# The grouped-query projection of the sample tiles as two times seven block products

## The chip, the cores and the metric

The kernel runs on one core of a Trainium2 chip. The metric is the device time of one execution, in microseconds. Before the change it was 1909.35 us (median of 3 runs, 1907.31 to 1909.38).

## What is computed

Two layers of a transformer step on 384 tokens of width 1024: one tile of 128 prompt tokens and two tiles of 128 sample tokens. Everything is float32. Cut to what matters here:

```python
z = h @ p['w_in']            # (384, 1024) @ (1024, 6048): all projections of the layer
(c_q, c_kv, k_pe, gq, gk, gv, dq, dk, dv, g_mla, g_gqa, g_diff) = jnp.split(z, splits, axis=-1)
gq = rmsnorm(gq.reshape(b, t, 8, 64), p['gqa_q_norm'])     # grouped-query: 512 columns of q,
gk = rmsnorm(gk.reshape(b, t, 2, 64), p['gqa_k_norm'])     # 128 of k, 128 of v: 768 in all
gv = gv.reshape(b, t, 2, 64)
o_mla, o_gqa = attend(q, k_mla, v_mla), attend(gq, gk_all, gv_all)      # 8 and 8 heads
a1, a2 = attend(dq[..., :64], ...), attend(dq[..., 64:], ...)           # 4 heads, two maps
merged = sigmoid(g_mla) * (o_mla @ w_br_mla) + sigmoid(g_gqa) * (o_gqa @ w_br_gqa) + ...
x = x + gate1 * (merged @ p['w_out'])
x = x + gate2 * expert_choice_ffn(h, p)                    # 16 experts, 3 matrices of 1024x1024 each
```

The change is in how the 768 grouped-query columns of `z` are computed for the 256 sample tokens.

## The kernel before

**Stages of a layer.** First the modulation and the normalised tokens, transposed into `hT` (8 blocks of 128 features by 384 tokens). Then the projection `c0` (latent attention), the grouped-query projection `c1` of the prompt tile, the q and v projections, and after that a loop over 16 attention jobs (`JOBS`: 8 `mla`, 4 `gqa`, 4 `diff`). Then the merge, the output projection, routing, and 16 experts, whose weights (12 MB each) stream through the 8 slots of `ring` and 10 more slots in `arena`.

**The job loop.** TensorE in job i does `scores(i)`, `prep(i + 1)` (transposes for the next job), `values(i - 1)`, then the filler list `FILL[i]`, then `turn_probs(i)` (transposes of the probabilities). VectorE does the maxima, ScalarE the exponentials, VectorE the normalisation; the filler gives TensorE work meanwhile. I write F0, F1, ... for the stretch of filler in job 0, 1, ... The order is written out by hand in `FILL`: F0 and F1 hold the `c1` projections of sample tiles 1 and 2 (`("c1", t, h)`, h the half of 384 columns), F2 and the lists after it other projections of `z`, the modulation blocks `ada` and their transposes `adat`, and the block products below.

**Block products.** `product` (L1849) and `two` (L1870) already compute other projections by seven products instead of eight: both operands are split into 2x2 blocks, and sums and differences of blocks are multiplied (M5, M1, M2, M6, M3, M7, M4, in this order). Each product is 4 accumulating matmuls of 192 columns. GpSimd makes the sums of blocks: `tile_sums` (L733) those of the tokens, `column_sums` (L743) those of the weights. ScalarE copies M5 and M1 out of their banks, VectorE adds the other five into place (L1339 to L1350). A plain projection (`project`, L1812) is 8 accumulating matmuls of 384 columns for a tile and a half, and ScalarE copies it out (L996).

**PSUM banks.** There are 8. Banks 0 to 3 hold scores. Banks 4 and 5 are used by `prep`: 4 for keys (copied out by VectorE, signal `prep_dve`), 5 for queries (copied out by ScalarE, `prep_act`); a filler may borrow them after that copy, and must be out before `turn_probs` takes them. Banks 6 and 7 are free for fillers. Every use is a "user", and `user_banks` gives it the bank used longest ago, by the numbers in `latest`; the user then waits until the former holder was copied out (`user_act` or `user_dve`).

**Weights.** SyncE's queue loads 1 MB units in the order of `PLAN` into the ring; a load waits until TensorE has counted the slot as used. The four `c1` units are released in the last projection of tile 2 (F1), and their slots take `ada` units that are used in F3.

**Signals.** `sq2_ok` comes after the squares of the latent projection, whose scratch `SQG` lies over columns 3072 to 4991 of `arena`; ScalarE squares the grouped-query rows into the same scratch at the end of F1 (L1076), with VectorE's mean and GpSimd's scaling after it (`rg_ok`).

## Time and profile before

| What | Value |
|---|---|
| median of 3 runs | 1909.35 us (1907.31 to 1909.38) |
| the profiled execution, its own time | 1909.12 us |
| its span, first to last instruction | 1907.3 us |
| TensorE matmul busy | 1760.6 us (92%) |
| VectorE / ScalarE / GpSimd busy | 671.7 / 325.6 / 320.7 us |
| mean granted TensorE clock | 0.986 |
| DMA | 541.14 MB, mean 284 GB/s |

The span ends 1.8 us short of the profiled execution's time; what lies around it is the start and the end of the program. A row of the trace names a line, an engine, an operation and its tiles. A float32 matmul shows as two records on PE and two weight loads on PEld, so that "x32" on PE is 16 matmuls. Arrows name what the engine waited for. The busy time of PE overlaps with the next records at its ends by some 0.1 us, so durations of stretches are best taken from start to start.

### The profile page before, as it was taken

The page shows a single profiled execution, that of the slowest core. Times are in us where ns is not written, and L with a number is a line of the kernel's source. Part 1 is how long each engine was busy: PE and PEld are TensorE (multiplying, and loading weights), DVE is VectorE, ACT ScalarE, POOL GpSimd, SP SyncE. Part 2 cuts the span into 40 slices and gives each one's busy share as a digit, 9 for nine tenths or more (in the row PEclk, how much of TensorE's full clock was granted, in tenths as well). Part 3 has the DMA queues.
Part 4 walks back from the last instruction along what each step waited for, and adds up shares of the span by engine and source line. Part 5 has one row for each costly group of instructions (what it writes and reads, how often), then busy time and mean ns, then how long its engine had stood idle before and what let it go on. Part 6 is the DMA issues. An engine that isn't in the chain of part 4 may idle for free.

```text
span 1907.3 us, 21463 instructions
## 1 busy us (share of the span) xinstructions
PE 1760.6 (92%) x8548; PEld 972.3 (51%) x8548; DVE 671.7 (35%) x1375; ACT 325.6 (17%) x811; POOL 320.7 (17%) x349
## 2 busy tenths in 40 slices
PE   6999999999999988889889999999999999898886
PEld 3656777894533323233255587778844333332322
DVE  1135556752412212122132455567424131221212
ACT  2232223320301001010032322222112010100101
POOL 0216455330000000000002437533200000000000
PEclk9999999999899999999999999999999999999999
DMA  9235132139499999999961642313448999999997
GB/s 389 84 143 235 70 130 78 67 136 412 184 428 427 431 428 429 430 429 429 427 246 71 236 159 94 122 46 131 196 202 331 429 430 428 430 429 429 428 429 294
DMA packets 58289, 541.14 MB, mean 284 GB/s; under 512 B 7048, under 2 KB 7496, under 8 KB 14416
## 3 DMA queue, kind: packets, MB, share of 16 engines
q1 hardware_dynamic: 56656, 535.65, 67.7%
q0 software_dynamic: 1536, 4.13, 0.6%
q8 instruction: 69, 1.13, 0.2%
q14 instruction: 28, 0.23, 0.0%
HBM read 536.54 MB, written 3.21 MB: 283 GB/s over the span
## 4 chain that ended last, share of the span: by engine, by line
PE 78%; DMA 12%; DVE 4%; SPq 3%; ACT 2%; issue 1%; DVEq 0%; ACTq 0%
PE banks L2300 25%; PE banks L1863 10%; PE banks L1825 8%; DMA arena<-in_w_exp 7%; PE banks L1915 7%; PE banks L2219 4%; PE banks L1717 4%; PE banks L1887 4%; SPq L678 3%; PE banks L2379 3%; DMA ring<-in_w_exp 3%; PE banks L2088 1%; PE banks L2275 1%; DMA ring<-in_w_att 1%; PE banks L1772 1%; PE banks L2029 1%
## 5 line engine op out<-in xcount | busy, mean ns | idle before, releaser
L2300 PE MATMUL banks<-arena 128*64 128x512 f32 x1680 | 378.9, 595 | 31.5 <-DMA arena<-in_w_exp 19.7
L2300 PE MATMUL banks<-ring,arena 128*64 128x512 f32 x1392 | 314.9, 598 | 21.0 <-DMA ring<-in_w_exp 10.9
L2300 PEld LDWEIGHTS banks<-arena 128*64 128x64 f32 x1680 | 116.6, 137 | 272.2 <-issue 217.5
L2300 PEld LDWEIGHTS banks<-ring,arena 128*64 128x64 f32 x1392 | 97.7, 138 | 220.9 <-issue 179.4
L1654 DVE TENSOR_TENSOR arena<-banks,arena 32x512 f32<-32x512 f32 (+1 forms) x128 | 87.9, 687 | 266.0 <-PE banks L2300 264.6
L1825 PE MATMUL banks<-ring,arena 128*128 128x384 f32 (+1 forms) x512 | 161.7, 476 | 1.8 <-ACT arena L930 1.8
L1717 PE MATMUL banks<-arena 128*128 128x128 f32 (+3 forms) x740 | 106.2, 278 | 31.5 <-DVE arena L1639 18.6
L1717 PEld LDWEIGHTS banks<-arena 128*128 128x128 f32 (+3 forms) x740 | 83.0, 140 | 94.0 <-issue 41.3
L1825 PEld LDWEIGHTS banks<-ring,arena 128*128 128x128 f32 x512 | 97.2, 192 | 61.7 <-issue 2.7
L1915 PE MATMUL banks<-arena,ring 128*128 128x384 f32 x384 | 126.8, 488 | 0.0
L1138 ACT ACTIVATE arena<-banks 128x512 f32<-128x512 f32 x32 | 19.1, 597 | 511.7 <-PE banks L2300 511.7
L806 POOL COPY arena<-arena 128x32 f32<-128x32 f32 x4 | 0.8, 211 | 604.6 <-ACT arena L1036 604.3
L1863 PE MATMUL banks<-ring 128*128 128x192 f32 x544 | 97.0, 328 | 0.8 <-DVE arena L1319 0.8
L1915 PEld LDWEIGHTS banks<-arena,ring 128*128 128x128 f32 x384 | 72.2, 190 | 48.8 <-issue 1.5
L1639 DVE TENSOR_TENSOR arena<-arena,banks 128x512 f32<-128x512 f32 x32 | 22.0, 688 | 207.4 <-PE banks L2300 207.4
L1863 PEld LDWEIGHTS banks<-ring 128*128 128x128 f32 x544 | 88.9, 190 | 3.5 <-DVE arena L1319 1.3
L2219 PE MATMUL banks<-ring,arena 128*128 128x512 f32 x192 | 86.5, 604 | 1.2 <-DVE arena L1319 1.2
L956 ACT ACTIVATE arena<-banks,arena 128x384 f32<-128x384 f32 x144 | 71.4, 508 | 91.0 <-DVE arena L1259 91.0
L1636 DVE TENSOR_TENSOR arena<-banks,arena 128x512 f32<-128x512 f32 x32 | 22.1, 691 | 171.8 <-ACT arena L1138 171.8
L908 POOL TENSOR_TENSOR arena<-arena 128x1024 f32<-128x1024 f32 x1 | 2.4, 2365 | 443.3 <-DVE arena L1664 443.3
L2379 PE MATMUL banks<-arena 128*128 128x512 f32 (+1 forms) x112 | 54.4, 642 | 21.7 <-DVE arena L1654 18.6
L1257 DVE TENSOR_REDUCE arena<-banks 128x1 f32<-128x384 f32 x144 | 58.5, 461 | 29.0 <-PE banks L2022 14.6
(251 smaller groups left out, 2051.5 us busy)
## 6 DMA issues: line engine op xcount, KB each, us to landing
arena<-in_w_exp SPq DMA_DIRECT2D x69, 2048.0 KB, 30.6
ring<-in_w_exp SPq DMA_DIRECT2D x69, 2048.0 KB, 29.5
ring<-in_w_att SPq DMA_DIRECT2D x80, 1024.0 KB, 6.7
arena<-in_w_exp SPq DMA_DIRECT2D x72, 1024.0 KB, 27.2
ring<-in_w_exp SPq DMA_DIRECT2D x36, 1024.0 KB, 14.1
ring<-in_w_att SPq DMA_DIRECT2D x26, 768.0 KB, 8.2
arena<-in_w_att SPq DMA_DIRECT2D x12, 1024.0 KB, 11.5
ring<-in_w_att SPq DMA_DIRECT2D x8, 672.0 KB, 15.2
```

The costliest lines, as they stand in the source:

```text
L678: sp.dma_start(span(group), a["w_exp"][l, c0:c1].rearrange("(p n) -> p n", p=P))\
L956: ins = nc.scalar.activation(PB[:, b, lo:hi], PS[:, 2 * m + bank, c:c + hi - lo], ACT.Exp, scale=SCALE[kind], bias=NB[:, b, r:r + 1], accu ...
L1257: ins = nc.vector.reduce_max(MX[:, b, r:r + 1], PS[:, 2 * m + bank, c:c + w], AX)
L1654: ins = nc.vector.tensor_tensor(y[32 * e:32 * e + hi - lo, BF * h:BF * h + BF], PS[64 * h + lo:64 * h + hi, 5], G2[64 * h + lo:64 * h + hi ...
L1717: return pe.transpose(out, src, IDT[0:rows, 0:rows])
L1825: ins = pe.matmul(ps[:, 0:width], hT[:, k, P * t:P * t + P], slots[n][:, c0:c0 + width], start=k == 0, stop=k == KC - 1)
L1863: ins = pe.matmul(ps[:, 0:HALF], lhs[:, k], rhs[:, k], start=k == 0, stop=k == 3)
L1887: ins = pe.matmul(ps[:, 0:HALF], lhs[:, k], rhs[k], start=k == 0, stop=k == 3)
L1915: ins = pe.matmul(ps[:, 0:TOK], w[:, k, P * (c % 4):P * (c % 4) + P], o[:, k], start=k == 0, stop=k == 3)
L2219: ins = pe.matmul(ps, MG[:, k, P * t:P * t + P], slots[n][:, c0:c0 + BF], start=k == 0, stop=k == KC - 1)
L2300: ins = pe.matmul(PS[64 * h:64 * h + 64, bank], lhs(k), slots[i][:, c0:c0 + BF], start=k == 0, stop=k == KC - 1)
L2379: ins = pe.matmul(combine_bank(g, n)[:, c:c1], w, YS[0 if t else 1][:, BF * h + c:BF * h + c1], start=True, stop=True)
```

## The change

The four `c1` projections of the sample tiles go out of F0 and F1. In their place stand two groups of seven block products, `("two", 2, q, m)`, q the half of 384 output columns: q = 0 in F0, q = 1 in F1. GpSimd gets two new pieces of work in each layer: `tile_sums(l, 1)` ahead of the rotary key, and `grouped_sums(l, q)`, the weight sums, q = 0 before the stores of the latent projection, q = 1 after the rotation of q. The sums of q = 1 go to the same four tiles (`WG`, arena columns 3072 to 6143) as those of q = 0, each after the product of q = 0 that reads it. ScalarE's squares wait for VectorE's last product of q = 1 instead of ScalarE's own last copy. In `user_banks` the estimates for when banks 4 and 5 become free change, and `("adat", 1)` is put in bank 4.

```diff
@@ fill table and bank assignment
-for _t in range(1, NT):
-    FILL[_t - 1] += [("c1", _t, h) for h in range(2)]
...
+GROUPED = 2
+for _q in range(2):
+    FILL[_q] += [("two", GROUPED, _q, m) for m in PRODUCTS]
...
         if left and left == len(FILL[i]):
-            latest[4], latest[5] = n - 1.6, n - (1.7 if i == 7 else 1.5)
+            late = 0 if i and values_of(i - 1) else 1
+            latest[4], latest[5] = n - 1.6 + late, n - 1.5 + late
             holder.pop(4, None), holder.pop(5, None)
-        b = min((4, 5, 6, 7) if left > 2 else (6, 7), key=lambda x: latest[x])
+        b = 4 if user == ("adat", 1) else min((4, 5, 6, 7) if left > 2 else (6, 7), key=lambda x: latest[x])
@@ backbone: operand tiles
-        TS = (SUMS[0][0], SUMS[0][1], at(25568, 4, P), SUMS[0][2])
+        TS = [(SUMS[0][0], SUMS[0][1], at(25568, 4, P), SUMS[0][2]),
+              (at(23264, 4, P), at(23776, 4, P), at(24288, 4, P), SUMS[0][2])]
+        WG = tuple(at(3072 + 4 * HALF * n, 4, HALF) for n in range(4))
@@ GpSimd
-            def tile_sums(l):
-
-                pool.wait_ge(user_mm.s, user_mm.at(l, USER_AT["gate", 0, 3, M4] + 1))
+            def tile_sums(l, early):
+
+                if early:
+                    pool.wait_ge(ht_act.s, ht_act.at(l, 4 * NT))
+                    pool.wait_ge(ht_dve.s, ht_dve.at(l, 4 * NT))
+                    pool.wait_ge(mod_t.s, mod_t.at(l, 1))
...
+            def grouped_sums(l, q):
+
+
+                units = [place[l, ("c1", u)] for u in range(4)]
+                for i, first, load, _ in units:
+                    pool.wait_ge(filled[first].s, 16 * load)
+                b11, b12 = ([columns(units[u][0], q, h) for u in range(2)] for h in range(2))
+                b21, b22 = ([columns(units[u][0], q, h) for u in range(2, 4)] for h in range(2))
+                t1, t2, t3, t4 = ([t[:, 0:2], t[:, 2:4]] for t in WG)
+                if q == 0:
+                    pool.wait_ge(sq2_ok.s, sq2_ok.at(l, 1))
+                else:
+                    pool.wait_ge(user_mm.s, user_mm.at(l, USER_AT["two", GROUPED, 0, M5] + 1))
+                pool.tensor_tensor(t1[0], b12[0], b11[0], ALU.subtract)
+                link(pool.tensor_tensor(t1[1], b12[1], b11[1], ALU.subtract), l)
+                if q:
+                    pool.wait_ge(user_mm.s, user_mm.at(l, USER_AT["two", GROUPED, 0, M6] + 1))
+                pool.tensor_tensor(t2[0], b22[0], t1[0], ALU.subtract)
+                link(pool.tensor_tensor(t2[1], b22[1], t1[1], ALU.subtract), l)
+                if q:
+                    pool.wait_ge(user_mm.s, user_mm.at(l, USER_AT["two", GROUPED, 0, M4] + 1))
+                for u in range(2):
+                    pool.tensor_tensor(t3[u], b22[u], b12[u], ALU.subtract)
+                pool.tensor_tensor(t4[0], b21[0], t2[0], ALU.subtract)
+                pool.tensor_tensor(t4[1], b21[1], t2[1], ALU.subtract).then_inc(two_ok.s, 1)
...
-                    pool.wait_ge(mod_t.s, mod_t.at(l, 1))
+                    pool.wait_ge(user_mm.s, user_mm.at(l, USER_AT["two", GROUPED, 1, M4] + 1))
...
+                tile_sums(l, 1)
                 pool.wait_ge(user_act.s, user_act.at(l, evacuated(USER_AT["c0", 2, 1])))
...
+                grouped_sums(l, 0)
 
                 pool.wait_ge(za_ok.s, za_ok.at(l, 1))
...
+                grouped_sums(l, 1)
                 pool.wait_ge(rg_ok.s, rg_ok.at(l, 1))
...
@@ ScalarE and VectorE
-                        act.wait_ge(user_act.s, user_act.at(l, evacuated(USER_AT["c1", 2, 1])))
+                        act.wait_ge(user_act.s, user_act.at(l, evacuated(USER_AT["c1", 0, 1])))
+                        act.wait_ge(user_dve.s, user_dve.at(l, evacuated(USER_AT["two", GROUPED, 1, M4])))
                         nc.scalar.activation(SQG, ZG[:, :, 0:640], ACT.Square).then_inc(sqg_ok.s, 1)
...
-                    c = 768 * b + TOK * u
-                    first, second = ZD[:, 1, c:c + TOK], ZD[:, 2, c:c + TOK]
+                    c, z = (TOK * u, ZG) if b == GROUPED else (768 * b + TOK * u, ZD)
+                    first, second = z[:, 1, c:c + TOK], z[:, 2, c:c + TOK]
@@ TensorE: two() and fill()
-                units = [arrived(l, "c2", 4 * f + u) for u in range(4)]
+                early = int(f == GROUPED)
+                units = [arrived(l, "c1", u) if early else arrived(l, "c2", 4 * f + u) for u in range(4)]
                 if m == M5:
-                    pe.wait_ge(tiles_ok.s, tiles_ok.at(l, 1))
-                    pe.wait_ge(two_ok.s, two_ok.at(l, 2 * f + q + 1))
+                    pe.wait_ge(tiles_ok.s, tiles_ok.at(l, 2 - early))
+                    pe.wait_ge(two_ok.s, two_ok.at(l, q + 1 if early else 2 * f + q + 3))
                 a11, a12, a22 = hT[:, 0:4, P:2 * P], hT[:, 4:8, P:2 * P], hT[:, 4:8, 2 * P:TOK]
                 b11, b21, b22 = ([columns(units[u + k // 2], q, h)[:, k % 2] for k in range(4)]
                                  for u, h in ((0, 0), (2, 0), (2, 1)))
-                t1, t2, t3, t4 = ([t[:, k] for k in range(4)] for t in WT[q])
-                s1, s2, s3, s4 = TS
+                t1, t2, t3, t4 = ([t[:, k] for k in range(4)] for t in (WG if early else WT[q]))
+                s1, s2, s3, s4 = TS[early]
...
-                    project(l, key, [("c1", u) for u in range(4)], ZG_W, 384, 384 * key[2], key[1],
-                            key[1:] == (2, 1))
+                    project(l, key, [("c1", u) for u in range(4)], ZG_W, 384, 384 * key[2], 0, False)
```

Four more numbers follow from this: `DVE_LINKS` 139 to 143, `POOL_LINKS` 58 to 64, and the counts of `tiles_ok` and `two_ok` (2 and 6), with the waits in `two` that go by them.

**TensorE, F0** (job 0 of a layer, between the transposes for job 1 and those of the probabilities of job 0). Before:

```order
L1717 MATMUL banks<-arena 96x128 x3
L1825 MATMUL banks<-ring,arena 128x384 x16
L1717 MATMUL banks<-arena 128x128 x7
L2020 MATMUL banks<-arena 128x384
L2021 MATMUL banks<-arena 128x128
L2022 MATMUL banks<-arena 128x384
```

Now:

```order
L1756 MATMUL banks<-arena 96x128 x3
L1927 MATMUL banks<-arena 128x192 x4
L1927 MATMUL banks<-ring,arena 128x192 x8
L1927 MATMUL banks<-arena 128x192 x4
L1927 MATMUL banks<-ring,arena 128x192 x4
L1927 MATMUL banks<-arena 128x192 x8
L1756 MATMUL banks<-arena 128x128 x7
```

Sixteen matmuls of 384 columns gave way to 28 of 192; F1 reads the same.

**GpSimd, from the rotation of q to the scaling of the grouped-query rows**, with the signals each instruction waits for. Before:

```order
L731 TENSOR_TENSOR arena<-arena 128x8x32 [waits pool_chain]
L835 TENSOR_TENSOR arena<-arena 128x640 [waits qrope_ok,rg_ok]
L836 TENSOR_TENSOR arena<-arena 128x512 [waits pool_chain]
L838 TENSOR_TENSOR arena<-arena 128x128
L835 TENSOR_TENSOR arena<-arena 128x640 [waits pool_chain]
```

Now:

```order
L735 TENSOR_TENSOR arena<-arena 128x8x32 [waits pool_chain]
L765 TENSOR_TENSOR arena<-ring 128x384 [waits filled7,filled6,user_mm,filled1,filled5]
L766 TENSOR_TENSOR arena<-ring 128x384
L769 TENSOR_TENSOR arena<-ring,arena 128x384 [waits user_mm,pool_chain]
L770 TENSOR_TENSOR arena<-ring,arena 128x384
L774 TENSOR_TENSOR arena<-ring 128x384 [waits user_mm,pool_chain]
L774 TENSOR_TENSOR arena<-ring 128x384
L775 TENSOR_TENSOR arena<-ring,arena 128x384
L776 TENSOR_TENSOR arena<-ring,arena 128x384
L873 TENSOR_TENSOR arena<-arena 128x640 [waits qrope_ok,rg_ok]
```

The eight additions of q = 1 stand between them, with three waits for TensorE (`user_mm`).

**TensorE, F7** (job 7, the products of the first gate), with the signals. Before:

```order
L1863 MATMUL banks<-ring 128x192 [waits tokens_ok,sums_ok,filled4,user_dve]
L1863 MATMUL banks<-ring 128x192 x3
L1863 MATMUL banks<-arena,ring 128x192 [waits filled4,prep_act]
L1863 MATMUL banks<-arena,ring 128x192 x3
L1863 MATMUL banks<-arena,ring 128x192 [waits filled4,prep_dve]
L1863 MATMUL banks<-arena,ring 128x192 x3
L1863 MATMUL banks<-ring 128x192 [waits filled4,user_dve]
```

Now:

```order
L1902 MATMUL banks<-ring 128x192 [waits tokens_ok,sums_ok,filled4,user_dve]
L1902 MATMUL banks<-ring 128x192 x3
L1902 MATMUL banks<-arena,ring 128x192 [waits filled4,user_dve]
L1902 MATMUL banks<-arena,ring 128x192 x3
L1902 MATMUL banks<-arena,ring 128x192 [waits filled4,prep_dve]
L1902 MATMUL banks<-arena,ring 128x192 x3
L1902 MATMUL banks<-ring 128x192 [waits filled4,prep_act]
```

The product M1 no longer waits for ScalarE's copy of bank 5 (`prep_act`); the fourth product, M6, has that wait now.

## Rows read from the trace of the kernel before

**Rows 1.** The page: DMA busy tenths, 40 slices of 47.7 us.

```profile
DMA  9235132139499999999961642313448999999997
```

**Rows 2.** Windows: stretch, length, busy us per engine, granted clock, DMA share, GB/s.

```profile
488.00:508.00 20.00, 17.65 (x61) 8.64 (x59) 10.84 (x31) 3.94 (x8) 0.00 (x0) 0.91 0.00 1
484.00:524.00 40.00, 37.05 (x171) 22.52 (x170) 20.39 (x63) 11.84 (x24) 0.00 (x0) 0.83 0.35 138
1424.00:1464.00 40.00, 35.90 (x216) 21.43 (x216) 21.21 (x66) 11.96 (x25) 4.01 (x8) 0.91 0.72 273
```

**Rows 3.** Timeline, TensorE, F0 and F1 of layer 0: start, us, work [idle before].

```profile
99.85 10.48 PE L1825 MATMUL banks<-ring,arena 128*128 128x384 f32 x32
110.17 0.93 PE L1717 MATMUL banks<-arena 128*128 128x128 f32 x7
...
114.49 10.49 PE L1825 MATMUL banks<-ring,arena 128*128 128x384 f32 x32
...
124.82 0.93 PE L1717 MATMUL banks<-arena 128*128 128x128 f32 x7
```

**Rows 4.** Chain that ended last, by time: 56 matmuls of `two` in F8.

```profile
221.31 18.20 PE banks L1887 x112
```

**Rows 5.** Timeline and waits, GpSimd: rotation of q, and the scaling's wait.

```profile
88.04 0.72 POOL L724 TENSOR_TENSOR arena<-arena 128x256 f32<-128x256 f32 x1 [17.72 <-ACT arena L1052]
...
POOL arena L835 <- DVE arena L1453: 41.1, 1, 41.1
```

**Rows 6.** Timeline after F7: TensorE goes on, GpSimd wakes, sums of four adds.

```profile
204.64 1.15 PE L1717 MATMUL banks<-arena 128*128 128x128 f32 x9
...
204.89 1.27 POOL L738 TENSOR_TENSOR ring<-arena 128x512 f32<-128x512 f32 x1 [15.72 <-PE banks L1863]
...
222.65 1.96 POOL L761 TENSOR_TENSOR arena<-ring 128x384 f32<-128x384 f32 x2
...
225.52 1.00 POOL L763 TENSOR_TENSOR arena<-ring,arena 128x384 f32<-128x384 f32 x1
```

**Rows 7.** Timeline after F1: squares, ScalarE's copy of probabilities, TensorE.

```profile
125.53 1.80 ACT L1076 ACTIVATE arena<-arena 128x1920 f32<-128x1920 f32 x1
...
127.24 0.46 ACT L1083 COPY arena<-banks 128x384 f32<-128x384 f32 x1
...
127.75 0.53 PE L1717 MATMUL banks<-arena 128*96 128x128 f32 x3 [0.49 <-ACT arena L1083]
```

**Rows 8.** Timeline, TensorE, F5 of layer 0: M5; M1, M2; M3; M7, M4.

```profile
167.19 1.47 PE L1863 MATMUL banks<-ring 128*128 128x192 f32 x8
...
168.84 2.87 PE L1863 MATMUL banks<-arena,ring 128*128 128x192 f32 x16 [0.18 <-DVE arena L1268]
...
172.84 1.46 PE L1863 MATMUL banks<-arena 128*128 128x192 f32 x8
...
174.31 2.87 PE L1863 MATMUL banks<-ring 128*128 128x192 f32 x16
```

**Rows 9.** Timeline, F7 of layer 0: M5; VectorE's key copies; M1, M2.

```profile
193.84 1.47 PE L1863 MATMUL banks<-ring 128*128 128x192 f32 x8
...
194.61 2.79 DVE L1274 COPY arena<-banks 64x512 f32<-64x512 f32 x4
...
196.74 2.87 PE L1863 MATMUL banks<-arena,ring 128*128 128x192 f32 x16 [1.43 <-ACT arena L967]
```

**Rows 10.** Timeline, TensorE, F4: `ada` 2 in layer 0; its end in layer 1.

```profile
158.09 2.80 PE L1796 MATMUL banks<-ring,arena 128*32 128x256 f32 x48 [1.28 <-ACT arena L979]
161.81 1.07 PE L1796 MATMUL banks<-ring,arena 128*32 128x256 f32 x16 [0.92 <-DMA ring<-in_w_att]
...
1100.77 0.70 PEld L1796 LDWEIGHTS banks<-ring,arena 128*32 128x32 f32 x16 [0.16 <-DMA ring<-in_w_att]
```

**Rows 11.** Timeline: one GpSimd add and one small VectorE multiply beside each other's work.

```profile
158.63 2.73 POOL L794 TENSOR_TENSOR ring<-ring 128x512 f32<-128x512 f32 x1 [3.13 <-issue]
...
209.62 0.62 DVE L1259 TENSOR_SCALAR arena<-arena 128x3 f32<-128x3 f32 x1
```

More of the change, by code:

```diff
@@ L399, in packed_vectors @@
     return out
-DVE_LINKS = 139
-POOL_LINKS = 58
+DVE_LINKS = 143
+POOL_LINKS = 64
 def backbone(nc, a):
@@ L731, in rotate @@
                 return pool.tensor_tensor(z, t1, t2, ALU.add)
-            def tile_sums(l):
-                pool.wait_ge(user_mm.s, user_mm.at(l, USER_AT["gate", 0, 3, M4] + 1))
+            def tile_sums(l, early):
[4 more added lines that the diff above has]
+                else:
+                    pool.wait_ge(user_mm.s, user_mm.at(l, USER_AT["gate", 0, 3, M4] + 1))
                 a11, a12, a21, a22 = hT[:, 0:4, P:2 * P], hT[:, 4:8, P:2 * P], hT[:, 0:4, 2 * P:TOK], hT[:, 4:8, 2 * P:TOK]
-                s1, s2, s3, s4 = TS
+                s1, s2, s3, s4 = TS[early]
                 link(pool.tensor_tensor(s1, a21, a22, ALU.add), l)
@@ L741, in tile_sums @@
                 pool.tensor_tensor(s4, a12, s2, ALU.subtract).then_inc(tiles_ok.s, 1)
+            def grouped_sums(l, q):
[7 more added lines that the diff above has]
+                    pool.wait_ge(sq2_ok.s, sq2_ok.at(l, 1))
+                else:
+                    pool.wait_ge(user_mm.s, user_mm.at(l, USER_AT["two", GROUPED, 0, M5] + 1))
[11 more added lines that the diff above has]
+                pool.tensor_tensor(t4[1], b21[1], t2[1], ALU.subtract).then_inc(two_ok.s, 1)
             def column_sums(l, f, q):
```

6 lines of the change are left out of this document (3 added, 3 removed).

## The prediction

> **What bounds the kernel now.** I read the 40 slices first. The DMA row has two long runs of 9, the experts of each layer, and low digits between them [rows 1]. So there are two kinds of stage: attention, where TensorE's own queue sets the pace, and experts, where the weight stream does. An edit in attention pays only if the stream behind it starts earlier too. Between the two, from 488 to 508 us, the DMA share is 0.00 [rows 2]: all slots that may be filled are full, and the stream waits for TensorE to use some. So it starts when attention and routing are done, and what attention gains should reach the end one for one. The second view is the chain by time with the timeline of TensorE in F0 and F1, where the projections stand back to back [rows 3]; the reader should see that start-to-start times there hold no idle. The third is the timeline of the later fills, where short waits sit inside the products [rows 8 to 10].
>
> **The fills themselves.** F0 takes 110.17 - 99.85 = 10.32 us, F1 124.82 - 114.49 = 10.33 [rows 3]: 16 matmuls of 384 columns at 0.645. In F8 the same kind of products, 56 matmuls of 192, take 18.20 us [rows 4], 0.325 each, 1.30 a product, so 28 take 9.10. Saved: 2 x (10.32 - 9.10) = 2.45 us a layer. It is nearly the whole of the eighth that seven products for eight leave out; the short matmuls cost next to nothing extra.
>
> The Trainium skill ("TensorE: Matmul & The Clock Gate", Back-to-back issue gap) speaks against that: in a stream of weight loads and matmuls it gives about 81 ns for 128 columns and 131 for 512, so half the columns would cost far more than half the time. The trace disagrees: 0.325 against 0.645 us. The rival "short matmuls" below has this direction, with a bound from the rows.
>
> **Do the products of F0 and F1 wait?** M2 borrows bank 4 and M6 bank 5, 2.6 and 3.9 us into the fill. In F7 bank 5 came free 196.74 - 193.84 = 2.9 us into it [rows 9], and in F5 bank 4 168.84 - 167.19 = 1.65 us into it [rows 8]; both come in time. M3 and M7 take over the banks of M5 and M1, M4 that of M3, two products earlier each. The copies and adds are ScalarE's and VectorE's, hidden as those of the gate products are. Cost 0; if VectorE came late in M3's add, M4 would wait by as much.
>
> **GpSimd.** The token sums are four adds at the size of L738, 1.27 us [rows 6]: 5.1 us, ahead of the rotary key, while GpSimd has nothing else. The eight adds of q = 0 take 2 x 3.87 = 7.7 us, with 3.87 from 222.65 to 225.52 + 1.00 for four [rows 6]. They stand before the stores and the rotation of q; GpSimd had 17.72 us of idle there [rows 5]. With each add doubled they would still fit. So 0; behind them wait only the two stores and that rotation, which wakes on ScalarE's last copy at 88.0 anyway.
>
> The sums of q = 1 are the tight place. Their t3 and t4 may be written only after M4 of F0, and M5 of F1 waits for all four tiles. From the end of the fill to M5 there are 114.49 - 110.17 = 4.32 us of other TensorE work [rows 3]. GpSimd wakes 0.25 us after TensorE goes on (204.64 to 204.89) and needs 3.87 for four adds [rows 6]: 4.12, and a signal back of about 0.1 us or a little more. M5 starts then or some tenths later. I take 0.1 us a layer. Lower bound 0. Upper: an add that meets VectorE's work took 2.73 us instead of 1.27 [rows 6, 11]; two of four such would make it 2.9 late, one 1.4. The scaling behind these adds is not delayed: it waited 41.1 us for VectorE [rows 5].
>
> The Trainium skill ("SBUF — State Buffer", Who interferes with whom) says VectorE and GpSimd share a port pair under an exclusive lock: the loser blocks for the whole instruction. The trace agrees: the 2.73 us add, and a three-column multiply of VectorE that took 0.62 us beside a GpSimd add [rows 11]. By that rule the small multiply before job 1's exponentials loses about half a microsecond too, off TensorE's path, since the fill covers it.
>
> **The squares.** After F1 ScalarE does 1.8 us of squares from 125.53, then the copy at 127.24 for which TensorE idles 0.49 us at 127.75 [rows 7]. The squares started 0.71 us after the fill's end (124.82, behind the copy of the last projection). Now they wait for VectorE's last add of 192 columns. VectorE should wake as GpSimd does, 0.25 us after the fill [rows 6], and I give the add 0.35, half of the 0.70 that one of four key copies of 512 columns takes [rows 9]: 0.6 us after the fill. Gain about 0.12 a layer; bounds 0 and 0.49.
>
> **The banks of the later fills.** F5: M1 started at 168.84 where 167.19 + 1.30 = 168.49 was possible, waiting for VectorE's key copy in bank 4; now M1 is in bank 7 and only M2 needs bank 4, later than that copy: 0.35. M7 started at 174.31, with 172.84 + 1.30 = 174.14 possible, as its bank was M6's, emptied by VectorE just before; now it is M1's: 0.17 [rows 8]. Together 0.52.
>
> F7: M1 waited 1.43 us for ScalarE's copy of bank 5 [rows 9]. Now M1 has bank 6 and does not wait, but M2 has bank 4 as before, and VectorE's four key copies end at 194.61 + 2.79 = 197.40. So the next wait stands right behind: M2 starts at 197.46 instead of 196.74 + 1.30 = 198.04. Gain 0.58, not 1.43.
>
> F4: `ada` 2 waited 1.28 us for ScalarE's copy of the values of job 3 [rows 10], since its bank had held them; now its bank was `ada` 1's. But its last quarter then waits for weights: 0.92 us in layer 0, and in layer 1 the weight load still waited 0.16 us for DMA at 1100.77 [rows 10]. These loads are issued as `ada` 1 frees slots, so their arrival does not move. I take 0; the bounds are 0 and 1.28 a layer. The earlier release of the `c1` slots doesn't help: the loads that it starts are used two jobs later.
>
> **The sum.** A layer: 2.45 - 0.10 + 0.12 + 0.52 + 0.58 = 3.57; two layers 7.1 us. The profiled execution took 1909.12 us: 1902.0. Its time is 0.23 below the median of the runs, so I forecast 1902.2.
>
> **Rivals.**
>
> *Short matmuls.* Each matmul has a fixed cost that doesn't shrink with its columns, and these products have 28 where the projections had 16. At the far end a short one costs what a long one does, 28 x 0.645 = 18.1 us a fill instead of 9.1: four fills make 36 us, 1938. It costs the whole gain from 0.325 + 7.1 / 112 = 0.39 us a matmul. [Rows 4] speak against it, with the same shapes at 0.325. Chance 0.01.
>
> *The sums make F1 wait.* If one or two adds of q = 1 are held up, M5 is 1.4 to 2.9 us late a layer: 1904.8 to 1907.8. For it: adds beside VectorE at [rows 11]. Against: in those 4 us VectorE mostly reads banks, and its large multiplies fall into the middle of the fills. Chance 0.12.
>
> *The gain is swallowed at the expert stage.* The clock granted to TensorE was 0.83 from 484 to 524 us in layer 0 and 0.91 over the same stretch of layer 1 [rows 2], after idle stretches in routing: 40 x 0.17 = 6.8 and 40 x 0.09 = 3.6 us of full-speed work lost. So the same work loses 3 us more or less by how its idle falls. A layer that goes from one to the other moves the time by up to 3 us, either way: 1899 or 1905. Chance of the bad side 0.12, of the good side 0.1.
>
> *F4 pays after all*, if the loads come earlier: up to 2.6 us more, 1899.6. Chance 0.07.
>
> *Slower than before.* GpSimd and VectorE lock each other out in F0 and F1: every one of the four adds after M4 takes 2.73 us as at [rows 11]. Then the tiles are ready at 0.25 + 10.9 = 11.2 us, 6.9 after TensorE wants them, and each layer loses 6.9 - 3.6 = 3.3 us: 1915.7. It decides from 3.7 us of lateness a layer on, where the change breaks even; that takes three of the four adds held up by VectorE. Chance 0.03.
>
> *The order is not what it says*: no sign, the listing of the instructions shows the 28 matmuls and the additions where I put them.
>
> **Chances.** Main forecast 0.55, with its own range of 1900.5 to 1903.7. Change and no change differ by 0.2%, 3.8 us, the least that runs of this kernel can tell: faster means below 1905.5. That holds the main case, the good sides, half of the waits in F1 and most of the bad clock: 0.82. Within 0.2%: 0.14. Slower: 0.04, with room for what I don't see. The range runs from the good clock or F4's gain to the upper end of the late sums.
>
> **What would show it.** In the profile after: F0 at 9.1 us start to start and F1 too; in F1 M5 with a wait for GpSimd of under 0.5 us; L765 to L776 on GpSimd with adds near 1.0 us; no wait of M1 in F5 and F7, but one of about 1.0 us of M2 in F7 for VectorE's key copies; `ada` 2 with a longer wait for DMA and the same end; layer 1 beginning some 3.6 us earlier. Wrong would be: M5 of F1 over 1.5 us late, an expert stream that starts no earlier than before, or `ada` 2 ending earlier.

## The result

The changed kernel took 1896.83 us (median of three runs, 1896.20 to 1899.92) against 1909.35 before: ratio 0.9942, 95% interval 0.9924 to 0.996. The profiled execution took 1896.20, with a span of 1894.4. The forecast was 1902.2, and its range began at about 1899, the good clock; so this is below the range. Two more comparisons, with five runs of the changed kernel each, gave 1901.03 against 1908.88 (ratio 0.9963, 0.995 to 0.9975) and 1901.38 against 1908.85 (0.9961, 0.9949 to 0.9974). All 15 runs of the changed kernel have a mean of 1900.6, all 65 of the kernel before 1908.9: 8.4 us less, with a 95% interval of about 1.5 to either side. So there are two questions: where the 8 us are, and why the first three runs showed 12.5.

### The stages of the profile after

The rows below are all of TensorE's timeline in layer 0 of the changed kernel (start, us, work, idle before with its releaser). First F0 and the start of F1, beside [rows 3]:

```profile
97.50 1.47 PE L1927 MATMUL banks<-arena 128*128 128x192 f32 x8
98.80 2.76 PE L1927 MATMUL banks<-ring,arena 128*128 128x192 f32 x16
...
106.60 0.93 PE L1756 MATMUL banks<-arena 128*128 128x128 f32 x7
...
110.93 1.52 PE L1927 MATMUL banks<-arena 128*128 128x192 f32 x8
112.29 2.76 PE L1927 MATMUL banks<-ring,arena 128*128 128x192 f32 x16
...
120.09 0.93 PE L1756 MATMUL banks<-arena 128*128 128x128 f32 x7
```

F0 takes 106.60 - 97.50 = 9.10 us and F1 120.09 - 110.93 = 9.16, where they took 10.32 and 10.33. M5 of F1 starts 4.33 us after the end of F0 as before, and takes 1.36 us to the next product, 0.06 longer than the 1.30 of the others. GpSimd's last sums are as close as this:

```profile
106.91 1.95 POOL L774 TENSOR_TENSOR arena<-ring 128x384 f32<-128x384 f32 x2 [1.83 <-PE banks L1927]
108.83 0.99 POOL L775 TENSOR_TENSOR arena<-ring,arena 128x384 f32<-128x384 f32 x1
109.78 0.99 POOL L776 TENSOR_TENSOR arena<-ring,arena 128x384 f32<-128x384 f32 x1
```

They end at 110.77, 0.16 us before M5. The longest of the eight adds of q = 1 takes 1.11 us; none is stretched to 2.73 as the one at [rows 11] was. Next the squares, F4, F5 and F7, beside [rows 7 to 10]:

```profile
122.96 0.53 PE L1756 MATMUL banks<-arena 128*96 128x128 f32 x3 [0.43 <-ACT arena L1122]
...
146.63 1.06 PE L1811 MATMUL banks<-ring,arena 128*32 128x512 f32 x8 [0.48 <-DMA ring<-in_w_att]
...
152.63 2.80 PE L1835 MATMUL banks<-ring,arena 128*32 128x256 f32 x48
156.58 1.07 PE L1835 MATMUL banks<-ring,arena 128*32 128x256 f32 x16 [1.15 <-DMA ring<-in_w_att]
...
161.97 1.47 PE L1902 MATMUL banks<-ring 128*128 128x192 f32 x8
163.27 2.76 PE L1902 MATMUL banks<-arena,ring 128*128 128x192 f32 x16
...
168.47 2.76 PE L1902 MATMUL banks<-ring 128*128 128x192 f32 x16
171.07 0.93 PE L1756 MATMUL banks<-arena 128*128 128x128 f32 x7
...
187.90 1.47 PE L1902 MATMUL banks<-ring 128*128 128x192 f32 x8
189.20 1.46 PE L1902 MATMUL banks<-arena,ring 128*128 128x192 f32 x8
191.51 1.57 PE L1902 MATMUL banks<-arena,ring 128*128 128x192 f32 x8 [0.84 <-DVE arena L1313]
...
198.11 1.15 PE L1756 MATMUL banks<-arena 128*128 128x128 f32 x9
```

The reader should see four things. The wait behind the squares is 0.43 where it was 0.49. F4 has lost its wait for ScalarE (1.28), but the wait for weights behind it has grown from 0.92 to 1.15, and F3 has one of 0.48 that it did not have. F5 has no wait and takes 9.10 (9.82 before). In F7 M1 goes at once and M2 waits 0.84 for VectorE's key copies: 10.21 instead of 10.80.

From the start of F0 to the end of F7 that is 198.11 - 97.50 = 100.61 us where it was 204.64 - 99.85 = 104.79: 4.18 less. Layer 1 took 103.66 and now takes 99.94 (1032.16 to 1132.10): 3.7 less. Together 7.9 us. The stages behind pass it on one for one. In layer 0 the routing matmuls that stood at 494.72 are at 488.16, which is the 6.5 us by which F7 ended earlier. So the other 12.9 - 7.9 = 5 us of the span are not in the projections at all.

### Where the other 5 us are

The first half of them is there before the first grouped-query product: it starts at 97.50 instead of 99.85, although nothing ahead of it on TensorE was changed. The windows show the reason for most of it. The columns are stretch, length, busy us by engine, granted clock of TensorE, DMA share, GB/s. The kernel before:

```profile
20.00:40.00 20.00, 15.99 (x84) 8.33 (x77) 5.58 (x19) 3.48 (x9) 0.00 (x0) 0.83 1.01 414
```

The changed kernel:

```profile
20.00:40.00 20.00, 17.18 (x93) 8.54 (x86) 5.62 (x19) 5.32 (x14) 0.00 (x0) 1.00 1.02 418
```

A mean of 0.83 over 20 us says that a third of them was granted the lower of the two levels, 1.2 instead of 2.4 GHz; the changed kernel shows 1.00, none. From the first sample-tile matmul to the first product they took 65.87 and 64.18 us. Ahead of that matmul 24 transposes took 3.39 and 2.84 us. The second place is routing: up to the four transposes at 507.97 and 499.88 it took 13.24 and 11.73 us (from 494.72 and 488.16).

The third is late in the experts of layer 1, and it isn't the clock. From 1602.58 in the kernel before (1590.91 now) it took 53.55 and 52.26 us, with a granted clock of 1.00 in both; what differs is the wait for weights, first before and then now:

```profile
1639.87 3.65 PE L2300 MATMUL banks<-ring,arena 128*64 128x512 f32 x16 [0.33 <-DMA ring<-in_w_exp]
1644.70 3.65 PE L2300 MATMUL banks<-arena 128*64 128x512 f32 x16 [1.18 <-DMA arena<-in_w_exp]
```

```profile
1631.73 3.65 PE L2339 MATMUL banks<-arena 128*64 128x512 f32 x16 [0.43 <-DMA arena<-in_w_exp]
```

Behind it a stretch at half speed made 29.0 us of 27.3 in the kernel before (from 1763.41, now 1750.33), but the 101.4 us that follow are 103.2 now, since the weights are waited for again: that half speed had cost next to nothing by the end. In all, 0.66 us lie ahead of the first sample-tile matmul (0.55 of them in those transposes), 1.69 between it and the first product, 1.5 in routing and 1.3 in the experts of layer 1, less 0.2 in those of layer 0. Whether this belongs to the change or to the execution was the question for the experiments.

The windows of [rows 2] in the changed kernel say little by themselves, since their stretches now hold work that stood 7 to 12 us later:

```profile
484.00:524.00 40.00, 37.04 (x182) 21.36 (x180) 20.79 (x65) 12.24 (x25) 0.00 (x0) 0.87 0.51 209
1424.00:1464.00 40.00, 35.58 (x229) 19.67 (x230) 16.29 (x47) 9.74 (x20) 4.01 (x8) 0.91 0.86 350
```

The clock is 0.87 and 0.91, against 0.83 and 0.91. The DMA row of the page answers to [rows 1]: its two runs of 9 have the same number of slices, so the expert stages are as long as they were to within a slice, 47 us.

```profile
DMA  9246222149499999999961642312548999999997
```

### The profile page after: what moved, and what is told of

Its sections match the earlier page's. It is cut to its first block, busy times and chain, and to the rows that moved or that the text cites. A ratio compares the mean times of both kernels' runs of the same rounds, so it can differ in the third digit from the quotient of the medians.

```text
span 1894.4 us, 21814 instructions
## 1 busy us (share of the span) xinstructions
PE 1750.6 (92%) x8644; PEld 981.5 (52%) x8644; DVE 686.7 (36%) x1403; ACT 323.5 (17%) x811; POOL 361.6 (19%) x389
## 3 DMA queue, kind: packets, MB, share of 16 engines
q8 instruction: 70, 1.15, 0.2%
## 4 chain that ended last, share of the span: by engine, by line
PE 77%; DMA 12%; DVE 4%; SPq 3%; ACT 2%; issue 1%; DVEq 0%; ACTq 0%
PE banks L2339 25%; PE banks L1902 10%; DMA arena<-in_w_exp 8%; PE banks L1955 7%; PE banks L1864 6%; PE banks L1927 6%; PE banks L1756 4%; PE banks L2258 4%; SPq L682 3%; PE banks L2418 3%; DMA ring<-in_w_exp 3%; DMA ring<-in_w_att 2%; PE banks L2127 2%; PE banks L2314 1%; PE banks L2068 1%; PE banks L1811 1%
## 5 line engine op out<-in xcount | busy, mean ns | idle before, releaser
L1864 PE MATMUL banks<-ring,arena 128*128 128x336 f32 (+1 forms) x384 | 118.1, 468 | 1.8 <-ACT arena L968 1.8
L1864 PEld LDWEIGHTS banks<-ring,arena 128*128 128x128 f32 x384 | 72.3, 190 | 45.1 <-ACT arena L968 2.3
```

The lines of the kernel that those rows point to most:

```text
L1864: ins = pe.matmul(ps[:, 0:width], hT[:, k, P * t:P * t + P], slots[n][:, c0:c0 + width], start=k == 0, stop=k == KC - 1)
```

## The experiments

All ratios are to runs of the kernel before on the same chip. The stage times are start to start on TensorE, as above.

### The two kernels again

No edit; each was run a second time, and the changed one a third.

> The kernel before, unchanged. The mechanism theory (all that is systematic happens between the first grouped-query product and the end of the grouped-query projection; the rest of the difference between the two first profiles is where the granted TensorE clock happened to dip): ratio 1.000 to the kernel before, and this profile need not show the clock of 0.59 at 24 to 28 us and of 0.76 and 0.81 at 32 to 40 us again; first grouped-query matmul at 98 to 100 us. The systematic theory (the start is slower in the old program itself): that matmul again at 99.85 and the first sample-tile matmul at 33.98.

Measured: ratio 1.000 (0.9992 to 1.0009), 1909.47 us. The first sample-tile matmul is at 33.30, the first grouped-query fill at 97.67. That is 2.2 us earlier than in the first profile of the same program (and 0.3 earlier than the expected 98), so what the systematic theory wanted to see again is gone. Its F0 took 11.82 instead of 10.32, since half speed now fell there.

> The changed kernel, unchanged. Mechanism theory: 7.5 to 8.5 us less than the kernel before in the stretches of the two projections (104.79 and 103.65 to about 100.3 and 99.9), and a total between 1898 and 1902, since the other 5 us of the first comparison were the clock's: ratio 0.9955 to 0.997. Systematic theory: ratio 0.993 to 0.9945 again (1896 to 1899), with the first grouped-query matmul at 97.5 and the routing stretch 1.5 us shorter once more.

Measured: ratio 0.9963, 1901.03 us. The projections took 101.43 and 99.87, F0 of layer 0 among them 10.39, with half speed in it. The first product starts at 99.63, routing takes 13.24. The two projections are 7.1 us shorter, just under the expected 7.5 to 8.5, with 1.3 us of half speed in F0. So the mechanism theory holds, and the rival doesn't: neither the start nor routing is faster because of the change.

> The changed kernel once more, unchanged, for a third set of times and a third profile. Where the first comparison (12.5 us by medians, 12.9 by spans) and the second (7.9 us) differ, the theory is that the stretches at half of TensorE's clock fell elsewhere. It expects 7 to 9 us less than the kernel before (ratio 0.9953 to 0.9963), the stage times of layer 1 as in the two other profiles within 0.1 us (fills 9.10 and 9.17, F5 9.10, F7 10.21, sum 99.9), and every stage that is longer than in the other profiles by over 0.2 us under a half-speed stretch or a DMA wait. Rival (the first comparison was the true size): ratio 0.9935 and a mean granted clock of 0.988 or more in all runs.

Measured: ratio 0.9961, 1901.38 us; F0 10.48 with half speed in it, F1 9.16, F5 9.10, F7 10.22, the projection of layer 1 99.88, routing 13.24. All this was expected. One stage was not: the first sample-tile matmul is at 34.55, where it is at 33.3 and 33.4 in the two other profiles, and neither a low granted clock nor a wait for weights accounts for it. Up to 24.3 us this profile and the first one of the changed kernel agree to 0.03 us. Then come 24 transposes, here and in the first profile of the changed kernel:

```profile
26.17 3.92 PE L1756 MATMUL banks<-arena 128*128 128x128 f32 x24
```

```profile
26.01 2.84 PE L1756 MATMUL banks<-arena 128*128 128x128 f32 x24
```

And the window over them here:

```profile
25.00:30.00 5.00, 5.00 (x32) 3.68 (x24) 0.00 (x0) 0.00 (x0) 0.00 (x0) 1.00 1.02 420
```

The first of these transposes start 0.21 us apart, those from 28.35 on 0.11, and the granted clock reads 1.00 for both. So TensorE can run at half pace at the start of the program without a sign of it in that column.

### The parts alone

`banks_only` is the kernel before with these lines of the new one, and no grouped-query products (the `min` is written out in the change above):

```
+            late = 0 if i and values_of(i - 1) else 1
+            latest[4], latest[5] = n - 1.6 + late, n - 1.5 + late
+        b = 4 if user == ("adat", 1) else min(...)
```

> The kernel before with only the new rules for the accumulator banks of the fillers (no grouped-query products). Mechanism theory: F5 and F7 lose their waits (0.52 to 0.72 and 0.58 us per layer), F4 trades its wait of 1.28 us for a DMA wait of 1.14 (0 to 0.15), so 2.2 to 2.9 us less in the two stretches and a ratio of 0.9985 to 0.9989. Rival (F4's wait goes as well, since only the DMA's luck kept it): 4.5 to 5 us less, ratio 0.9975. Rival (banks cost through the squares and sums that now come later): 0 to 1 us less.

Measured: ratio 0.9987 (0.9978 to 0.9996), 1906.64 us. F5 takes 9.10 in both layers and F7 10.21, as in the changed kernel: 0.72 + 0.59 = 1.31 a layer. F3 and F4 together did not become shorter (18.48 in layer 0, with part of F4 at half speed; 17.10 in layer 1, where it was 16.96).

`products_only` is the changed kernel with the old bank rules from slot 2 on:

```
-            late = 0 if i and values_of(i - 1) else 1
-            latest[4], latest[5] = n - 1.6 + late, n - 1.5 + late
+            late = 1 if i < 2 else 0
+            latest[4], latest[5] = n - 1.6 + late, n - (1.7 if i == 7 else 1.5) + late
...
-        b = 4 if user == ("adat", 1) else min(...)
+        b = min(...)
```

> The changed kernel with the old rules for the banks of every filler from the third on: only the products of slots 0 and 1 and their sums are new. Mechanism theory: the two fills shorten by 1.2 us each, so 4.7 to 4.9 us less in the two stretches, ratio 0.9974 to 0.9976, and 1.5 per layer slower than the changed kernel in F5 and F7. If fills and banks together are the whole, this one and banks_only add up to the changed kernel within 1 us. Systematic theory: each of them shows part of the further 5 us, outside the two stretches, and their sum reaches 12.

Measured: ratio 0.9973 (0.9964 to 0.9982), 1903.75 us. F0 of layer 0 takes 9.10, F1 9.17 and 9.16; F5 and F7 have their old 9.82 and 10.80, which is 1.3 us a layer more than in the changed kernel (expected: 1.5), with the old wait of M1:

```profile
191.75 2.87 PE L1902 MATMUL banks<-arena,ring 128*128 128x192 f32 x16 [1.43 <-ACT arena L1005]
```

The two parts by medians are 5.1 and 2.2 us, 7.4 together, where the whole is 7.5 to 7.9 in the repeats. Each of these is good to some 2 us, so it is the stage times that show fills and banks to add up; neither part contains the further 5 us.

### F4 alone

`adat_only` is the kernel before with one line changed (which of the banks 6 and 7 later fillers get shifts with it):

```
-        b = min(...)
+        b = 4 if user == ("adat", 1) else min(...)
```

> The kernel before with one change: the accumulator bank of the transposed modulation tile is 4, as in the changed kernel (the choice between 6 and 7 of later fillers shifts with it). The prediction put this edit at nothing, since a DMA wait stands behind the ScalarE wait of 1.28 us at 158.09. Theory: the ScalarE wait goes and the DMA wait at the last 16 matmuls grows to about the sum, F3 and F4 together stay at 18.1 to 18.5 in layer 0 and 16.9 to 17.0 in layer 1, ratio 0.9995 to 1.0005. Rival: F4 pays, 0.5 to 1.28 us less in layer 0. If the products are what lets the weights of F4 come sooner (17.2 to 17.7 with them in three profiles, 18.1 to 18.5 without in three), this one is to stay on the side without.

Measured: ratio 1.0006 (0.9997 to 1.0015), 1910.18 us. TensorE's timeline in F4 of layer 0, for this kernel:

```profile
155.91 2.80 PE L1796 MATMUL banks<-ring,arena 128*32 128x256 f32 x48
161.17 1.32 PE L1796 MATMUL banks<-ring,arena 128*32 128x256 f32 x16 [2.46 <-DMA ring<-in_w_att]
```

In `before_again`, the same program but for this bank:

```profile
157.41 2.80 PE L1796 MATMUL banks<-ring,arena 128*32 128x256 f32 x48 [1.28 <-ACT arena L979]
161.35 1.07 PE L1796 MATMUL banks<-ring,arena 128*32 128x256 f32 x16 [1.14 <-DMA ring<-in_w_att]
```

1.28 + 1.14 = 2.42 became 2.46. The removed wait comes back as a wait for weights that were behind it, to a few hundredths. F3 and F4 of layer 0 together took 18.60, a little over the expected 18.1 to 18.5; the last row shows 1.32 us where 1.07 is full speed. In layer 1 they took 17.47 instead of 16.96, over the expected 17.0: the wait of 1.29 us went, and one of 1.47 for weights came, with matmuls ahead of it that took 2.98 instead of 2.80. So nothing was gained in either layer, and the ratio is just above the expected 1.0005.

### GpSimd's sums at F1

`sums_late` makes the third of the four sums of q = 1 (`t3`, two adds) twice:

```
+                if q:
+                    pool.tensor_tensor(t3[0], b22[0], b12[0], ALU.subtract)
+                    link(pool.tensor_tensor(t3[1], b22[1], b12[1], ALU.subtract), l)
                 for u in range(2):
                     pool.tensor_tensor(t3[u], b22[u], b12[u], ALU.subtract)
```

> The changed kernel, with GpSimd doing the third of the operand sums of the second grouped-query product twice (two more adds of 128 x 2 x 192 and one more link in each layer), so that the last sum is ready later by about 1.9 us. The prediction had put the last product of F1 0.05 us behind the sums, and the profile of the changed kernel shows that wait at 0.06 us. Theory (the sums have no slack at F1): M5 waits for GpSimd, and F1 grows from 9.17 by 1.5 to 2.1 us in each layer, 3 to 4.2 us in all, ratio 1.5 to 2.2 thousandths above the changed kernel's. Rival (the pages' small wait has slack behind it, since M1 could go first or the adds overlap): F1 grows by under 0.5 us.

Measured: ratio 0.9978 (0.9969 to 0.9987), 1905.10 us, against 0.9961 for the changed kernel in the same series: 1.7 thousandths, within the expected 1.5 to 2.2. The sums end at 116.89 + 0.99 = 117.88, first view, and TensorE takes the product up 0.15 us later, second view:

```profile
116.89 0.99 POOL L779 TENSOR_TENSOR arena<-ring,arena 128x384 f32<-128x384 f32 x1
```

```profile
115.69 0.49 PE L1759 MATMUL banks<-arena 128*96 128x128 f32 x3
118.03 1.54 PE L1930 MATMUL banks<-arena 128*128 128x192 f32 x8 [1.85 <-POOL arena L779]
```

From the end of F0 to M5 of F1 it is 6.34 us in both layers instead of 4.33: 2.01 us more. The sums end 6.19 us after F0 instead of 4.17: 2.02 more. So they have no slack, as the prediction had it. The expectation looked for the lateness inside F1; it stands ahead of M5, between F0 and F1, and F1 itself still takes 9.17.

### The other bank in F7

`other_bank_f7` is the changed kernel with the old constant for slot 7, so that M2 takes bank 5 and M6 bank 4:

```
-            latest[4], latest[5] = n - 1.6 + late, n - 1.5 + late
+            latest[4], latest[5] = n - 1.6 + late, n - (1.7 if i == 7 else 1.5) + late
```

> The changed kernel with one number back as it was: in slot 7 bank 5 counts as the older of the two turn banks, so that M2 takes bank 5 (released by a ScalarE copy) and M6 bank 4 (released by the VectorE copies at L1313). In the profile of the changed kernel M2 starts 3.61 us after F7's start, having waited 0.84 for those copies; in the kernel before, the bank that ScalarE releases was free 2.90 us after it. Theory: M2 waits 0.1 to 0.2 instead of 0.84, F7 takes 9.4 to 9.6 instead of 10.21 in both layers, 1.3 to 1.5 us less in all, ratio 0.7 thousandths below the changed kernel's. Rival (M6 or a later product then waits for bank 4 or for VectorE, which evacuates M2, instead): F7 stays at 10.0 to 10.3.

Measured: ratio 0.995 (0.9937 to 0.9962), 1899.05 us, against 0.9961 and 1901.38 for the changed kernel in the same series. F7 takes 9.50 us in both layers. TensorE in layer 0:

```profile
190.84 1.47 PE L1902 MATMUL banks<-ring 128*128 128x192 f32 x8
192.14 3.16 PE L1902 MATMUL banks<-arena,ring 128*128 128x192 f32 x16
195.14 1.46 PE L1902 MATMUL banks<-ring 128*128 128x192 f32 x8
```

Two products that follow each other without a wait take 2.60 from start to start; here M1 and M2 take 3.00. F7 is 0.71 us a layer shorter than in the changed kernel. The intervals of the two ratios overlap, so the whole times don't tell the two apart, but the stage times do: 9.50 twice, against 10.21 or 10.22 in both layers of five profiles. This version is faster than the kernel before by both, and better than the changed kernel by its stage.

### Four more profiles

Two of each kernel, unchanged.

> The changed kernel, one more profile, to see where TensorE's clock falls. Theory (the stretches at half speed fall by chance at the start, around the first grouped-query product, in the routing stage and late in the experts; nothing else differs between executions): the stage from the first sample-tile matmul to the first grouped-query product takes 64.2 us where no half-speed stretch lies in it and 65.5 to 66.5 where one does; F0 of layer 0 takes 9.10 or 10.4; the routing stretch 11.7 or 13.2; the sums of the projection in layer 1 stay 99.9. A time near 1896 needs the start and F0 free of half speed; near 1901 has one or both in it. Rival (the first comparison's 1896 is what the kernel does on a good chip): the times differ with no half-speed stretch to show for it.

> As for the look before it: the changed kernel, with 64.2 us or 65.5 to 66.5 from the first sample-tile matmul to the first grouped-query product, F0 9.10 or 10.4, and routing 11.7 or 13.2, each by whether a half-speed stretch lies in it; projection of layer 1 at 99.9.

> The kernel before, one more profile. By the same theory: 64.2 or 65.5 to 66.5 us to the first grouped-query fill, F0 of layer 0 10.32 or 11.5 to 11.8, routing 11.7 or 13.2, the projection of layer 1 103.7; F3 and F4 of layer 0 together 18.1 to 18.6 (17.2 to 17.8 in the changed kernel), if the products are what frees the weight blocks sooner.

> As for the look before it: the kernel before, with 64.2 or 65.5 to 66.5 us, 10.32 or 11.5 to 11.8, 11.7 or 13.2, and 103.7 us in the same four places, and 18.1 to 18.6 for F3 and F4 of layer 0.

Measured: 1896.71 and 1905.05 us for the same changed kernel, 1907.57 and 1908.08 for the kernel before. The stages of all profiles of the two kernels (an asterisk: a stretch with the granted clock at half speed lies within; the column after the span is the mean granted clock):

```
                 span  clock  to the 1st  F0 (0)  F3+F4 (0)  F0-F7 (0)  F0-F7 (1)  routing
before         1907.3  0.986    65.87*    10.32     18.08     104.80     103.66    13.24*
before_again   1904.6  0.987    64.37*    11.82*    18.32     106.52*    103.69    11.73
before_look4   1905.8  0.986    65.87*    10.32     18.26     104.97     103.66    13.25*
before_look5   1906.3  0.988    65.87*    10.32     18.29     104.99     104.98*   12.75*
after          1894.4  0.989    64.18      9.10     17.65     100.62      99.94    11.73
after_again    1899.2  0.986    66.26*    10.39*    17.17     101.43*     99.87    13.24*
after_third    1900.5  0.986    66.17*    10.48*    17.39     101.75*     99.88    13.24*
after_look4    1894.9  0.989    65.87*     9.10     17.25     100.22      99.84    11.73
after_look5    1903.3  0.985    66.32*    10.33*    17.26     101.47*    101.29*   13.24*
```

"To the 1st" is from the first sample-tile matmul to F0; (0) and (1) are the layers. Apart from F3 and F4, where weights are waited for, each of these stages has one value at full speed, equal to a few hundredths in all executions of a kernel, and a longer one where half speed lies in it. So for them the rival, times that differ with no half speed to show for it, is out.

Some of the expectations failed all the same. The projection of layer 1 was to stay at 99.9 and 103.7, but took 101.29 and 104.98 in the two last profiles, with half speed in its F0. Routing was to take 11.7 or 13.2 and took 12.75 in `before_look5`. A time near 1896 was to need a start free of half speed, but `after_look4` had it there (65.87) and took 1896.71. And outside these stages there is scatter that I haven't traced to the granted clock: the first sample-tile matmul is at 32.86 to 34.55 in the seven profiles that have no low clock ahead of it, and from the routing matmuls of layer 1 to the end it is 477.9 to 479.2 us, with the two kernels overlapping.

Half speed shows in the windows, first `after_look4` and then `after_look5` (columns as above):

```profile
84.00:104.00 20.00, 18.43 (x71) 11.65 (x70) 7.54 (x18) 5.29 (x14) 7.06 (x14) 1.00 0.00 1
484.00:508.00 24.00, 21.01 (x108) 12.35 (x106) 15.34 (x46) 8.80 (x16) 0.00 (x0) 1.00 0.17 61
```

```profile
84.00:104.00 20.00, 18.43 (x57) 10.87 (x56) 6.14 (x15) 5.27 (x14) 5.19 (x13) 0.91 0.00 1
484.00:508.00 24.00, 21.65 (x76) 10.18 (x76) 12.51 (x37) 6.96 (x14) 0.00 (x0) 0.89 0.00 2
```

And in the timeline of TensorE, the four matmuls of M5 in F0 and the two at the head of routing of `after_look5`, two records each:

```profile
101.07 2.69 PE L1927 MATMUL banks<-arena 128*128 128x192 f32 x8
...
492.62 3.66 PE L2258 MATMUL banks<-ring,arena 128*128 128x512 f32 x4
```

M5 takes 1.47 us in the profile after, and the two matmuls, there at 488.16, take 1.96.

In time at full speed (span times mean granted clock, good to about 1 us since the clock has three digits) the changed kernel comes to 1873.6, 1872.6, 1873.9, 1874.1 and 1874.8 in its five profiles, although the spans are up to 8.9 us apart; the kernel before to 1880.6, 1879.8, 1879.1 and 1883.4. The difference of the means is 6.9, and the first pair differs by 7.0 instead of 12.9. The Trainium skill ("TensorE: Matmul & The Clock Gate", Terms) prices time below full speed as that time by one minus the ratio of the clock. The five spans of the changed kernel agree with it to about 1 us. The four of the kernel before don't, being 4.3 us apart by it, and over all 15 runs of the changed kernel it gives 1868.6 to 1875.3: the mean clock also counts half speed that the wait for weights hides. So the stage times are the evidence, and the product of span and clock is a rough check. No run here shows what makes an execution fall into one pattern or the other.

## Why the prediction was right, and where it was wrong

**The forecast of the fills was right.** 2.45 us a layer were forecast, less 0.10 for M5's wait, 2.35; F0 and F1 gave 1.22 + 1.16 = 2.38 with the 0.06 of M5 in it. The rival of the short matmuls is refuted wherever F0 is free of half speed: 28 matmuls take 9.10 us. So is the slower case: the adds of GpSimd behind M4 of F0 take 1.00 or less each in both layers of the profile after.

**The term of F5 was too small.** Forecast 0.52, measured 0.72 a layer (9.82 to 9.10, `banks_only` alone too). I had counted the two waits that start-to-start times show at M1 and M7. The other 0.2 are in the two rows x16, two products each, 2.87 us long [rows 8], where two products without a wait have 2.76, as they now have here. 28 x 0.325 = 9.10 against the fill's 9.82 would have shown the whole.

**F7 was right in size and mechanism.** Forecast 0.58, measured 0.59. That M2 would wait for the key copies right behind stood in the prediction; `other_bank_f7` shows what that wait was worth. The squares gave 0.06 where I had 0.12.

**F4 was right as far as its bank goes, wrong on when its weights arrive.** The edit is worth nothing (`adat_only`). But "these loads are issued as `ada` 1 frees slots, so their arrival does not move" failed for layer 0, and `ada` 2 ended earlier, one of the prediction's own signs of being wrong. F3 and F4 together take 17.17 to 17.78 us in the eight profiles that have the products, and 18.08 to 18.60 in the six that don't: some 0.9 us, which the forecast put at 0 with a bound of 1.28. Layer 1 shows nothing of it: 16.96 to 17.00 in the four profiles of the kernel before, 16.88 to 16.96 in the five of the changed one. The last quarter of `ada` 2 waits for the sixth load that is issued behind F2. Its issue, in the kernel before and then in the changed one:

```profile
151.00 0.33 SPq L682 DMA_DIRECT2D ring<-in_w_att  x1
```

```profile
146.21 0.33 SPq L686 DMA_DIRECT2D ring<-in_w_att  x1
```

It lands at 161.76 and 156.54, and TensorE goes on at 161.81 and 156.58. F2 ends at 140.30 and 135.51, so it is issued 10.70 us behind F2 in both, and in all fourteen profiles to 0.01. What moved is the landing: 21.46 to 21.72 us behind F2 in the six profiles without the products, 3.6 to 4.0 after the load before it; 20.54 to 21.15 in the eight with them, 2.5 after it. The traces show one thing that goes with this in all fourteen: a packet of 16 KB of the kind `instruction`, 0.9 to 1.4 us long. Without the products it starts 17.7 to 18.2 us behind F2, beside the sixth load. With them it starts 6.2 to 6.5 behind F2, beside the second load, which then lands 5.5 to 6.1 us after the first instead of 5.1 to 5.4; that is the load for which F3 waits 0.48 us in the profile after. No run moved this packet alone, so that it makes the loads late is likely but not shown.

The prediction's other sentence, that the earlier release of the `c1` slots doesn't help, isn't contradicted. The changed kernel releases them in M1 and M3 of F1, and issues the six loads that take them from 113.13 on instead of 121.14 (the kernel before first):

```profile
121.14 5.32 SPq L682 DMA_DIRECT2D ring<-in_w_att  x6
```

```profile
113.13 6.18 SPq L686 DMA_DIRECT2D ring<-in_w_att  x6
```

But all six have landed 0.9 us behind F2 at the latest in either kernel, long before the sixth load of the next group is issued.

**The sum was 1.2 us short.** 3.57 a layer were forecast, 7.1 in all. The missing parts are F5's 0.2 a layer and the 0.9 of F3 and F4 in layer 0. At full speed layer 0 gained 104.92 - 100.42 = 4.5 (means of the executions without an asterisk) and layer 1 103.67 - 99.88 = 3.8, 8.3 in all. The runs together say 8.4. From 1909.1 that is 1900.8, inside the range, 1.4 below the forecast.

**The step that failed was the one on the clock.** The prediction set its sum against one profiled execution. It named one stage where the clock could fall otherwise, routing and the head of the experts, and gave it 3 us to either side: its good side, 1899, is where the range began. It left out the other stages, and it didn't add this good side to a sum that itself could be short. The profiles show four places: the warm-up before the first product (64.18 to 66.32), F0 of layer 0 (1.2 to 1.5 us), F0 of layer 1 (1.3 to 1.4) and routing (1.5). They are hit in changing combinations: `after` has none of the four, `after_look5` all of them, `before` the first and the last. The same program took 1896.71 and 1905.05 us.

In the first pair of profiles the 12.9 us between the spans are 7.9 of the projections, 3.7 of half speed (1.69 and 0.55 at the start, 1.5 in routing) and some 1.3 of a wait for weights in the experts of layer 1, which the prediction didn't have either and which scatters from execution to execution. The two other first runs of the changed kernel weren't profiled; their mean clock, 0.988, and the 0.989 of the first are at or above that of the ten runs of the two later comparisons, 0.984 to 0.988, which agrees with it but doesn't show it. So the 12.5 us of the first comparison are some 8 of the change and some 4 of what its executions happened to be. That the first three runs came out low was chance: the later medians, 1901.03 and 1901.38, lie inside the prediction's narrower range of 1900.5 to 1903.7. The direction of its good side was right and the size too small; the low end should have been near 1896.

## What to carry to other kernels

A stage whose work is unchanged tells how fast the execution was: compare those first, and put what they differ by aside before the rest is explained. A wait that is removed is worth only the distance to the next one behind it (0.59 of 1.43 in F7, nothing of 1.28 in F4), so look up who releases the second bank too: handing out the other one first gave 0.71 us a layer more. Where operand sums end 0.16 us before the product that reads them, every further add costs its whole length.

## What was not expected of the hardware

Two executions of one program on one core were 8.3 us apart (0.44%). In the stages of the table they differ by the placing and amount of half speed alone, 4.7 us; the rest lies ahead of the first sample-tile matmul (1.4 us) and between routing and layer 1's first product (2.2), where half speed differs too but isn't shown to be the whole of it. The 15 runs of the changed kernel went from 1896.20 to 1905.05, the 65 of the kernel before from 1905.83 to 1913.62, with standard deviations of 2.6 and 1.4 us; why the changed one scatters more is open. Half speed that falls in the stretch behind routing, ahead of the experts (from 500 to 526 us in the changed kernel), cost little: `after_look4` was 4.0 us faster there than the first profile of the changed kernel (21.59 against 25.56 us), and 3.0 of it were gone by the start of layer 1's work, since the experts between took 442.04 against 439.08 us. If the weight stream sets that stage's end, this is what it does. A load of 1 MB landed over 1 us late in each of the six profiles that had a packet of 16 KB of the kind `instruction` beside it.
